# Head transposes of odd query/key units in a second pair of PSUM banks

## The reference

```
def mla_queries(cq, q_a_norm, w_q_up, q_norm, rope):
    q = (rms_norm(cq, q_a_norm) @ w_q_up).reshape(B, L, H_MLA, MLA_QK)
    q = rms_norm(q, q_norm)
    if rope is not None:
        q = concatenate([q[..., :MLA_NOPE], apply_rope(q[..., MLA_NOPE:], rope)])

def mla_keys(ckv, k_rope, w_kv_up, k_norm, rope):
    kv = (ckv @ w_kv_up).reshape(B, L, H_MLA, MLA_NOPE + MLA_V)
    k_nope, v = kv[..., :MLA_NOPE], kv[..., MLA_NOPE:]
    k = rms_norm(concatenate([k_nope, broadcast(k_rope)]), k_norm)
    ...rope as for q where there is one

s = einsum('bqhd,bkhd->bhqk', q, k) * dq ** -0.5      # attention uses them
```

## Time and profile before

| | us |
|---|---|
| median of 3 executions | 1521.69 (1521.18 to 1524.51) |
| the profiled execution, its own time | 1522.7 |
| its span, first to last instruction | 1520.9 |
| PE busy | 1261.0 (83%) |
| DVE busy | 601.1 (40%) |
| ACT busy | 311.4 (20%) |
| POOL busy | 305.8 (20%) |
| mean granted TensorE clock | 0.924 |

### The profile page before, as it was taken

One profiled execution on the slowest core, in us unless ns is written; L12 is line 12 of the kernel. 1 busy time (PEld: TensorE's weight loads), 2 busy tenths in 40 slices (PEclk: granted clock), 3 DMA queues, 4 the chain that ended last, 5 costly groups with the idle time before them and its releaser, 6 DMA issues.

```text
span 1520.9 us, 20559 instructions
## 1 busy us (share of the span) xinstructions
PE 1261.0 (83%) x6795; PEld 782.9 (51%) x6796; DVE 601.1 (40%) x1364; ACT 311.4 (20%) x666; POOL 305.8 (20%) x703
## 2 busy tenths in 40 slices
PE   4999998778889759997772589999799679999764
PEld 3666775454457445553330366676566345555333
DVE  1211433556522442221110569999622622222215
ACT  3300144445400311111110320000221311111112
POOL 3000100200000013443333022142000033444330
PEclk9999999879989859999996699999999679999996
DMA  9566646210043049999999201110062179999965
GB/s 339 217 271 236 259 167 258 83 55 1 1 166 134 33 172 375 412 406 405 404 392 324 84 28 56 37 47 1 0 249 83 70 252 392 392 399 411 406 262 207
DMA packets 149091, 322.60 MB, mean 212 GB/s; under 512 B 16181, under 2 KB 49947, under 8 KB 142883
## 3 DMA queue, kind: packets, MB, share of 16 engines
q1 hardware_dynamic: 128432, 288.25, 49.9%
q0 software_dynamic: 12464, 21.91, 4.1%
q10 hardware_dynamic: 8131, 11.57, 2.1%
HBM read 312.41 MB, written 27.08 MB: 223 GB/s over the span
## 4 chain that ended last, share of the span: by engine, by line
PE 49%; DVE 16%; SPq 12%; DMA 9%; issue 6%; ACT 3%; POOL 2%; ACTq 1%; POOLq 0%; DVEq 0%
PE PS L585 9%; PE PS L634 8%; DVE arena L1953 8%; PE PS L938 7%; SPq L472 6%; SPq L469 5%; DMA ring<-in_moe_w_up 4%; PE PS L960 3%; PE PS L551 2%; PE PS L1022 2%; PE PS L805 2%; DMA arena<-y_rows 2%; DVE scratch L1449 2%; PE PS L1039 2%; PE PS L820 2%
## 5 line engine op out<-in xcount | busy, mean ns | idle before, releaser
L938 PE MATMUL PS<-arena 128*64 128x256 f32 x1152 | 134.7, 383 | 21.5 <-DMA arena<-in_moe_w_up 20.6
L585 PE MATMUL PS<-arena,ring 128*128 128x320 f32 x512 | 142.3, 442 | 11.1 <-ACT arena L1428 7.4
L1953 DVE SCALAR_TENSOR_TENSOR arena<-arena,vecT 128x655 f32<-128x655 f32 x181 | 151.1, 906 | 0.0
L1449 DVE TENSOR_TENSOR arena<-arena,PS 128x128 f32<-128x128 f32 (+1 forms) x85 | 27.0, 326 | 309.2 <-ACT arena L1370 302.9
L1022 PE MATMUL PS<-arena,ring 128*128 128x320 f32 x512 | 141.3, 437 | 8.3 <-ACT arena L1177 7.2
L938 PE MATMUL PS<-ring,arena 128*64 128x256 f32 x1056 | 128.3, 394 | 22.4 <-DMA ring<-in_moe_w_up 20.7
L634 PE MATMUL PS<-ring,arena 128*128 128x256 f32 (+1 forms) x640 | 140.3, 372 | 0.0
L634 PEld LDWEIGHTS PS<-ring,arena 128*128 128x128 f32 x640 | 114.7, 190 | 26.7 <-issue 13.4
L585 PEld LDWEIGHTS PS<-arena,ring 128*128 128x128 f32 x512 | 99.5, 195 | 53.6 <-issue 14.3
L1022 PEld LDWEIGHTS PS<-arena,ring 128*128 128x128 f32 x512 | 98.3, 192 | 50.1 <-issue 10.1
L938 PEld LDWEIGHTS PS<-arena 128*64 128x64 f32 x1152 | 80.1, 137 | 64.9 <-DMA arena<-in_moe_w_up 17.1
(11 more groups left out here) (317 smaller groups left out, 1624.9 us busy)
## 6 DMA issues: line engine op xcount, KB each, us to landing
ring<-in_moe_w_up SPq DMA_DIRECT2D x64, 1024.0 KB, 13.7
arena<-in_moe_w_up SPq DMA_DIRECT2D x64, 1024.0 KB, 13.7
ring<-in_ada_w SPq DMA_DIRECT2D x48, 1024.0 KB, 11.1
ring<-in_moe_w_down SPq DMA_DIRECT2D x32, 1024.0 KB, 15.3
arena<-in_moe_w_down SPq DMA_DIRECT2D x32, 1024.0 KB, 15.3
arena<-y_rows ACTq DMA_DIRECT2D x10, 1024.0 KB, 11.4
ring<-in_od_w_in SPq DMA_DIRECT2D x16, 512.0 KB, 6.2
ring<-in_ev_w_in SPq DMA_DIRECT2D x7, 1024.0 KB, 14.9
```

The costliest lines, as they stand in the source:

```text
L585: last = pe.matmul(PS[:, b + n, 0:SEG], w[:, k, c:c + P], src[:, tile(k), n * SEG:(n + 1) * SEG], start=(k == 0), stop=(k == KD - 1))
L938: last = pe.matmul(PS[i * BLK:(i + 1) * BLK, 0, 0:2 * P].rearrange("p (a n) -> p a n", a=2), xblk[:, k, :], w[:, k % 4, :, i * P:(i + 1) * P],
L1449: return dve.tensor_tensor(out, a, b, op)
L1953: dve.scalar_tensor_tensor(out=acc, in0=src, scalar=wc, in1=acc, op0=ALU.mult, op1=ALU.add).then_inc(ev("conv_v"), 1)
```

## The change

Odd units are turned into banks 6 and 7 in place of 4 and 5; even units stay in 4 and 5. So T(u-2) no longer waits for the evictions of unit `u-3` but for those of unit `u-4`, the last user of the same pair. The two first uses have waits of their own: T(0) keeps its wait for the retention's bank 4, and T(1) waits until the last latent has been taken from bank 6 (`lat_c`) and the last adaLN columns from bank 7 (`mod_c` at 6). ACT and DVE read the turned heads from the pair of that unit. No instruction is added, removed or moved on any engine.

```
+        def turned_bank(u):
+            return 4 + 2 * (u % 2)
...
                 if u >= 2:
                     pe.wait_ge(ev("qk_n"), u - 1)
-                    if u >= 3:
-                        pe.wait_ge(ev("hd_a"), u - 2)
-                        pe.wait_ge(ev("hd_v"), u - 2)
+                    if u >= 4:
+                        pe.wait_ge(ev("hd_a"), u - 3)
+                        pe.wait_ge(ev("hd_v"), u - 3)
+                    elif u == 2:
+                        pe.wait_ge(ev("norm_a"), 2 * NT)
                     else:
-                        pe.wait_ge(ev("norm_a"), 2 * NT)
+                        pe.wait_ge(ev("lat_c"), len(LATENT))
+                        pe.wait_ge(ev("mod_c"), 6)
                     raw = qkraw[:, (u - 2) % 3, :].rearrange("p (h n) -> p h n", h=HEADS)
                     for h in range(HEADS):
-                        last = pe.transpose(quad(4 + h // 4)[0:QK, h % 4, :], raw[:, h, :], ident)
+                        last = pe.transpose(quad(turned_bank(u - 2) + h // 4)[0:QK, h % 4, :], raw[:, h, :], ident)
...
-                    act.activation(dst[:, 0:4, col:col + P], quad(4)[0:QK], ACT.Copy, scale=gain) \
+                    act.activation(dst[:, 0:4, col:col + P], quad(turned_bank(u - 2))[0:QK], ACT.Copy, scale=gain) \
...
-                    dve.tensor_scalar(dst[:, 4:8, col:col + P], quad(5)[0:QK], gain, None, ALU.mult) \
+                    dve.tensor_scalar(dst[:, 4:8, col:col + P], quad(turned_bank(u - 2) + 1)[0:QK], gain, None, ALU.mult) \
```

## The result

The changed kernel took 1509.24 us (median of 7, 1501.61 to 1510.69) against 1521.69 (7 in the same comparison): ratio 0.9912, 95% interval 0.9896 to 0.9927. A second comparison gave 1506.74 against 1520.27, ratio 0.9915 (0.9893 to 0.9937). So it is 12.4 to 13.5 us faster. 1507.3 was forecast, 14.4 us less.

What follows compares the result with a forecast made beforehand. PE's transposes were taken to wait on DVE's eviction in a closed loop; 8.24 (rounds) + 2.99 (units 8 to 10) + 1.98 (end) + 1.2 (opening) = 14.4 us, from 1521.69 to 1507.3 us, range 1503.5 to 1511.5.

Steps and rivals of the forecast that it cites:

- The bound: PE's head transposes wait 16.2 us behind DVE's eviction, which stands behind the next norm; a closed loop of 10.69 us.
- The round: Head copies of units 4, 6 and 8: 6.57 us apart, not 10.69, set by ACT and DVE; two rounds gain 8.24.
- Units 8 to 10: Copy of unit 10 comes 6.37 us after that of unit 8, not 9.36; gain 2.99 us.
- The end: T(10) 4.66 us after the copy of unit 10, the attention's first product 2.80 later; gain 1.98 us.
- The opening: T(1) waits for the adaLN bias, starting at about 277.55, not 278.24; gain taken as 1.2 us.
- my outer bound: Opening: if the clock doesn't fall at all, M(4) ends at 281.2, 3.5 us earlier.
- The sum: Whole kernel: 13.21 us from rounds, units 8 to 10 and end, plus 1.2 from the opening: 14.4 us less.
- full clock sooner: Rival, attention: denser PE leaves the clock up, up to 3.6 us more gain, 1503.7 us; chance 0.06.
- The clock did not stay down through the stage: Rival, stage before the attention: clock stays at 1.2 GHz, attention 1.6 us later, up to 1526.9 us; chance 0.03.
- no other wait took the place of the one that is gone: Rival, T(odd): another wait stands at the same place, only the end gains, 1519.7 us; chance 0.03.
- Contention: POOL's rotation against DVE's norm: costs nothing by the rows; if they meet, up to 0.6 us in all.
- Passing through: From the attention to the kernel's end: nothing found that stays at its old time, so the gain passes one to one.

Runs made afterwards that it cites:

- early_one_pair: Kernel before with its one bank pair, DVE evicting at the front of its step and ACT ahead of the root: 1502.01 against 1520.27 us.
- early_two_pairs: The change plus early evictions, ACT ahead of the root and DVE at the front of its step: 1501.86 against the kernel before's 1520.27 us.
- old_end: The change, but T(9) and T(10) wait again for both evictions of units 8 and 9: 1508.3 us in one execution.
- one_round: The change's banks for odd units, but only T(3) has the shorter wait, all others the old one: 1515.92 us in one execution.
- banks_only: The change with the old waits kept, every T(u-2) waiting for both evictions of unit u-3: 1520.68 against the kernel before's 1520.27 us.
- filler: Kernel before with 24 identity transposes into unused bank 6 ahead of T(3), T(5) and T(7), waits unchanged: 1517.43 against 1519.59 us.

## Why the prediction held, point by point

- **The bound** was read rightly: a closed loop over DVE's program. An eviction stood there behind the norm of the newest unit, a transpose waited for that eviction, and behind the transpose waited the next product, which the next norm needs. early_one_pair shows it from the other side, with one pair.
- **The round** (6.57 forecast, 6.60 and 6.58 measured) and its owner, ACT and DVE, held. early_two_pairs confirms the owner: moving the two evictions, with PE's program as it was, shortened it to 6.3.
- **Units 8 to 10** (6.37 forecast): 298.62 - 292.26 = 6.36.
- **The end** (4.66 and 2.80 us, 7.46 together): 7.43. T(10) ran at half clock, as taken. The gain of 1.98 is right against the old end of this trace (2.01 measured), whose T(9) ran at full clock; against old_end, whose T(9) didn't, it is 2.85.
- **The opening** was the mis-sized term. T(1) came where forecast (5.64 us after T(0) by the rows, 5.65 measured). I took 1.2 us, from a clock that falls as in the trace before. Both traces of the change show it not to fall: 12.79 - 9.33 = 3.46 us, my outer bound. Where it fell (early_two_pairs, old_end) the copy stood at 10.77 and 10.66, still 2.0 to 2.1 less, more than the 1.4 that I had from the clock's return in another round. What I did not see is that moving one small operation on DVE would give another 1.84 us here. Two slips of the working changed nothing: by its own numbers M(4) would end at 283.0 and 281.0, not at 283.2 and 281.2, so the gains are 1.5 and 3.5.
- **The sum.** The stages of the two traces differ by 52.97 - 36.30 = 16.67 us, which is 13.21 and 3.46; the medians differ by 12.4 and 13.5. The intervals of the ratios are 11.1 to 15.8 us and 9.6 to 16.3 us, so 14.4 lies in both and 16.7 in neither. One part of the difference is on record: the trace before had a slow opening. With the old wait at T(1) the copy of unit 4 stood at 12.79 (before), 12.83 (one_round), 11.74 (banks_only) and 11.68 us (filler); with the change's wait at 9.33, 9.33, 10.66 and 10.77. The means differ by 2.2 us, not 3.46. Another 0.8 to 0.9 went in the attention. Together that would leave 14.5 to 14.6; that the medians show one or two less is within the intervals. Also filler gained more in its trace than in the median (5.2 and 2.2), 1.1 of it in the opening, which filler doesn't touch. Whether the clock falls in fewer rounds in other executions of the kernel before wasn't shown.
- **Luck.** That 14.4 came so near is in part luck. In the traces the opening gained 2.3 us more than I took. Two things that I had put at nothing stood against it: the trace before had a slow opening (1.2 us of it by the means above), and the attention took longer (0.8 to 0.9). The rounds and the end are no luck; they came out to 0.1 us.
- **The rivals.** The attention did not get its full clock sooner: the granted clock shows it at the half clock for 11.8 us in the change and for 10.2 us before. That fits the longer attention, but doesn't explain it alone, since old_end had 12.3 us of it and the shortest attention (104.1). The clock did not stay down through the stage (granted 1.00 from 275 to 300), and no other wait took the place of the one that is gone, but the one for `modT` at T(1).
- **Contention** of POOL and DVE cost nothing in the change, as forecast: 0.72 us. The margin was the forecast's 0.1 us: DVE's norm of unit 5 ends at 286.44 and the rotation starts at 286.55. With early evictions they do meet (1.04 us).
- **Passing through**: one to one but for the 0.8 to 0.9 us in the attention, within the 2 us by which the rest of the kernel varies anyway. From T(0) to the end it is 1249.0 us before and 1248.8 in banks_only, 1235.2 and 1232.9 in the change.

## What to carry to other kernels

When an engine waits for a buffer to be emptied, see where the emptying stands in the other engine's program before buying a second buffer: moved ahead of the work that depends on the waiting engine, one pair of banks gained more than two pairs with the old order. When a buffer is doubled into space that somebody else used, the first use inherits that user's wait; here waiting for a 0.18 us operation cost 1.8 us, beside a gain of 16.7 in the same traces. And a hole on TensorE can cost more than its length: count the half clock behind it, which in the rounds here was 1.7 us to a wait of 2.4.

## What the runs showed of the hardware

Whether TensorE's clock has fallen behind one and the same hole was not the same in each execution. Up to T(3) filler is the kernel before, with the same hole of 3.57 us ahead of T(1); there T(1) took 1.05 us, in the trace before 1.91. Up to T(9) old_end is the change, with the same hole of 2.90; there T(1) took 1.91, in both traces of the change 1.05. The rows of T(1) in filler and in old_end:

```profile
275.36 1.05 PE L793 MATMUL PS<-cst,scratch 128*96 128x128 f32 x8 [3.57 <-DVE arena L1685]
```

```profile
275.81 1.91 PE L799 MATMUL PS<-cst,scratch 128*96 128x128 f32 x8 [2.90 <-DVE modT L1459]
```

The Trainium skill (TensorE: Matmul & The Clock Gate, Part 1) says that the monitor runs free of the kernel; the runs agree in that the same PE program met both levels. Bank pairs 4 and 5 or 6 and 7 made no difference of their own (0.9999).
